# Two pairs of loads of a down projection are asked for before the last store of the up projection

## Chip, cores and metric

The kernel runs on one core of a Trainium2 chip. The metric is the device time of one execution in microseconds (us), as the median of several runs.

## The reference, cut to what matters

The function is one layer of a decoder trunk on 1024 positions of width 1024, in float32. A mixer with three branches comes first and is not touched here. The second half of the layer is a gated feed-forward block with a causal convolution over three positions:

```python
def conv_gated_ffn(h, w_up, conv_w, w_down):
    up = causal_depthwise_conv(h @ w_up, conv_w)
    gate, val = jnp.split(up, 2, axis=-1)
    return (jax.nn.silu(gate) * val) @ w_down
```

`w_up` is 1024 x 5632 and `w_down` is 2816 x 1024. The result is added to x.

## The kernel before, in words

The engines run their own programs and wait on each other by semaphores. TensorE (PE) multiplies. ScalarE (ACT) and VectorE (DVE) copy, scale and split. SyncE (SP) issues the transfers of this stage, in the order of its program, so a wait in SP's program holds every transfer behind it. Each float32 operand is split into a high part (ACT, a copy to the matmul's type) and a low part (DVE, the value less its high part), and each product is made of three matmuls: high by high, high by low, low by high.

**Up projection** (`UpProjection`). 2816 features are 22 tiles of 128, numbered 0 to 21 (`LAST` is 21). For each tile PE makes the products, ACT and DVE put the sums together, scale and convolve them (`convolve`, L1560 and L1563), ACT applies silu (`gate_silu`, L1509), DVE multiplies gate and value (`gate`, L1571), and SP stores the gated tile of 128 x 1024 in DRAM (`store`, L1444, to `scr_act`, 512 KB). The tail of a tile's work lies beside the products of the next tile.

**Down projection** (`DownProjection`). It has 44 steps: steps 0 to 21 make the left half of the output columns, steps 22 to 43 the right half. A step s takes one gated tile f = s mod 22 and 128 rows of half of `w_down`. `load` (L1614 to L1621) brings both from DRAM with two transfers of 512 KB and 256 KB, into the raw buffers `a_raw[s % 2]` and `w_raw[s % 2]`, so that there are two pairs of buffers. ACT and DVE split them: `split_a_hi` (L1637), `split_w_hi` (L1644), `split_a_lo` (L1648), `split_w_lo` (L1652), in two pairs of split buffers as well. PE then makes 24 matmuls (L1675 to L1677), three for each of eight banks of PSUM. The waits of a step are:

- `load(s)`, from step 2 on, waits until both low parts of step s-2 are made (the raw buffers are then free) and until the store of tile f has landed.
- `split_a_hi(s)` waits for the load, and from step 2 on until step s-2 has been multiplied.
- `step(s)` waits for the two low parts of step s.

After step 21 and step 43 DVE adds x, eight tiles of 256 KB that `load_x` (L1626) brings to `down_x`, and `write_out` (L1630) stores the result.

SP's program at the seam is, in order: the loads of steps 0 and 1, the store of tile 20, the store of tile 21, a wait for the last product of one kind of the up projection, eight transfers of x, and then the loads of steps 2, 3, 4 and so on. On ACT and DVE the splits of step 2 stand directly behind the convolution, silu and gate of tile 21.

Of the kernel before, what the change touches and what calls it, by code (L numbers as in the profile page):

```python
# [1371 lines left out]
def after(eng, sem, value):  # L1372

    if isinstance(value, int) and value <= 0:
        return
    eng.wait_ge(sem, value)


def looped(eng, first, last, body):

    body(0)
    with eng.Fori(first, last) as i:
        body(i)
# [296 lines left out]
def stage_combine_out_ffn(m):  # L1680
# [32 lines left out]
    down = DownProjection(m, up)  # L1713
# [13 lines left out]
    def tile_of(it, u):  # L1727
        return it * 2 + u // NB, u % NB

    with nc.Block() as block:  # L1730
        @block.sync
        def _(sp):
            def body(it):
                for u in range(UNITS):
                    d, n = tile_of(it, u)
                    after(sp, mul_done, it * UNITS + u - (UNITS - 1))
                    sp.dma_start(gate[u], gate_src[n][:, bass.ds(d, 1), :].rearrange("p a t -> p (a t)")).then_inc(gate_in[u], 16)
                    after(sp, lo_done, it * UNITS + u - 1)
                    sp.dma_start(raw[u % 2], branch_src[n][:, :, bass.ds(d * P, P)]).then_inc(w_in[u % 2], 16)
                    if isinstance(it, int) and u == 1:  # L1740
                        for k in range(2):
                            sp.dma_start(wo_raw[slot[k]], m.ins["w_out"][0, k * P:(k + 1) * P, :]).then_inc(wo_in[k], 16)
            looped(sp, 1, ITERS, body)
            sp.wait_ge(mul_done, ALL)
            sp.dma_start(rows, m.ins["x"][0].rearrange("(i p) d -> p i d", p=P)).then_inc(x_in, 16)
            for k in range(2, KD):
                if freed_by[k]:
                    sp.wait_ge(wo_lo_done, freed_by[k])
                if k == 4:
                    sp.wait_ge(sum_done, KD)  # L1750
                sp.dma_start(wo_raw[slot[k]], m.ins["w_out"][0, k * P:(k + 1) * P, :]).then_inc(wo_in[k], 16)
            sp.wait_ge(wo_lo_done, 4)
            up.load(sp, 0)
            for t in range(TT):
                sp.wait_ge(x_add, 2 * t + 2)
                sp.dma_start(m.scr_x[t * P:(t + 1) * P, :], rows[:, t, :]).then_inc(x_saved[t], 16)
            sp.wait_ge(out_mm, 2 * TT)
            up.load(sp, 1)
            for j in (1, 2, 3, 4):
                sp.wait_ge(t_lo[j], HK)  # L1760
            up.load(sp, 2)
            for i in range(1, LAST + 1):
                if i + 2 <= LAST:
                    sp.wait_ge(up.lo[4], i + 1)
                    up.load(sp, i + 2)
                if i == LAST:
                    for s in range(2):
                        down.load(sp, s)
                up.store(sp, i - 1)
            up.store(sp, LAST)  # L1770
            sp.wait_ge(up.mm[6], LAST + 1)
            for t in range(TT):
                down.load_x(sp, 0, t)
            for s in range(2, down.STEPS):
                down.load(sp, s)
                if s == down.FT + 1:
                    for t in range(TT):
                        down.write_out(sp, 0, t)
                if s == down.FT + 4:
                    for t in range(TT):  # L1780
                        down.load_x(sp, 1, t)
            for t in range(TT):
                down.write_out(sp, 1, t)
            sp.wait_ge(down.saved, 2 * TT * 16)
# [440 lines left out]
```

## Time and profile before

| what | value |
|---|---|
| median of 3 runs | 1687.22 us (1685.41 to 1688.19) |
| the profiled execution's own time | 1687.36 us |
| its span, from first to last instruction | 1685.6 us |
| mean granted TensorE clock over the span | 0.972 |
| PE matmuls | 7326, busy 1552.4 us (92% of the span) |
| DVE, ACT, GpSimd (POOL) busy | 870.1, 609.9, 123.0 us |
| transfers | 153.65 MB, mean 91 GB/s |

The times of instructions in the rows below are in microseconds from the start of the span. The clock is given as a share of the full 2.4 GHz. The share of DMA is the mean busy share of the core's 16 DMA engines.

### The profile page before, as it was taken

Reading aid. Unit: us, or ns where it says so; the run is one execution under the profiler, and the core shown is the slowest. Engines: PE = TensorE matmul, PEld = TensorE weight load, DVE = VectorE, ACT = ScalarE, POOL = GpSimd, SP = SyncE. Lnnn points to the kernel's source line nnn. Section 1 sums busy time; section 2 is a strip of 40 time slices with the busy share of each in tenths; the row PEclk is TensorE's granted clock in tenths of the full one; section 3 lists DMA queues with packets and bytes.
Section 4 is the critical chain, followed back from the end, with each engine's and each line's share of the span. In section 5 each row is a group of like instructions: output and inputs, shape, how many; then the busy total and the mean of one; then the engine's idle time right before and its main releaser. Section 6 shows DMA issues by size and latency. Waiting matters only on the chain. (4 is left out here: it accounts for less than half of the span.)

```text
span 1685.6 us, 19061 instructions
## 1 busy us (share of the span) xinstructions
PE 1552.4 (92%) x7326; PEld 1256.9 (75%) x7326; DVE 870.1 (52%) x1147; ACT 609.9 (36%) x997; POOL 123.0 (7%) x104
## 2 busy tenths in 40 slices
PE   5999999996989999885898978999999999799999
PEld 4899876665576676674677767888888888688887
DVE  4310343336275333873582547888778877333433
ACT  4310234441213453222451324555555555233222
POOL 1000230002041001200220000000000000000000
PEclk9999999998999999997899988999999999899999
DMA  5220230004122011210754112222223221544743
GB/s 189 72 90 1 65 91 26 25 26 134 34 63 69 26 32 37 92 36 10 252 187 159 75 50 63 89 87 88 76 76 99 76 88 63 178 147 150 244 139 141
DMA packets 126500, 153.65 MB, mean 91 GB/s; under 512 B 11530, under 2 KB 94397, under 8 KB 126141
## 3 DMA queue, kind: packets, MB, share of 16 engines
q1 hardware_dynamic: 126224, 152.40, 27.6%
q8 instruction: 57, 0.93, 0.2%
q14 instruction: 30, 0.25, 0.1%
q10 hardware_dynamic: 189, 0.08, 0.0%
HBM read 115.55 MB, written 36.31 MB: 90 GB/s over the span
## 5 line engine op out<-in xcount | busy, mean ns | idle before, releaser
L1586 PE MATMUL ps<-split_arena 128*128 128x512 f32 x1320 | 309.4, 391 | 3.3 <-DVE split_arena L2029 2.4
L489 PE MATMUL ps<-split_arena 128*128 128x512 f32 x1152 | 285.8, 400 | 27.9 <-ACT plain_arena L524 15.1
L1586 PEld LDWEIGHTS ps<-split_arena 128*128 128x128 f32 x1320 | 248.7, 189 | 56.1 <-DVE split_arena L2029 3.1
L489 PEld LDWEIGHTS ps<-split_arena 128*128 128x128 f32 x1152 | 213.5, 191 | 74.1 <-issue 26.1
L1675 PE MATMUL ps<-down_w,down_a 128*128 128x512 f32 x352 | 137.7, 391 | 10.6 <-DVE down_w L1652 10.6
L1676 PE MATMUL ps<-down_w,down_a 128*128 128x512 f32 x352 | 137.4, 390 | 0.0
L1677 PE MATMUL ps<-down_w,down_a 128*128 128x512 f32 x352 | 137.4, 390 | 0.0
L1586 PE MATMUL ps<-up_b,split_arena 128*128 128x512 f32 x528 | 130.0, 397 | 4.9 <-DVE split_arena L1514 4.9
L1648 DVE TENSOR_TENSOR down_a<-plain_arena,down_a 128x1024 fp32r<-128x1024 f32 x44 | 53.9, 1224 | 155.4 <-ACT down_a L1637 155.3
L1586 PEld LDWEIGHTS ps<-up_b,split_arena 128*128 128x128 f32 x528 | 101.5, 193 | 26.7 <-DVE split_arena L1514 5.2
L1637 ACT ACTIVATE down_a<-plain_arena 128x1024 fp32r<-128x1024 f32 x44 | 46.7, 1061 | 171.9 <-PE ps L1677 144.9
L690 DVE TENSOR_REDUCE stat<-ps 128x1 f32<-128x128 f32 (+3 forms) x64 | 48.4, 756 | 103.4 <-PE ps L617 103.3
L315 PE MATMUL ps<-split_arena 128*128 128x426 f32 (+1 forms) x256 | 94.0, 367 | 6.2 <-issue 2.6
L531 POOL TENSOR_TENSOR split_arena<-plain_arena,split_arena 128x1024 fp32r<-128x1024 f32 x24 | 59.4, 2474 | 498.1 <-ACT split_arena L513 498.1
L659 ACT ACTIVATE plain_arena<-ps,stat 128x128 f32<-128x128 f32 (+3 forms) x64 | 47.5, 743 | 131.0 <-DVE stat L690 131.0
L316 PE MATMUL ps<-split_arena 128*128 128x426 f32 (+1 forms) x256 | 92.4, 361 | 0.0
L317 PE MATMUL ps<-split_arena 128*128 128x426 f32 (+1 forms) x256 | 92.2, 360 | 0.0
L1675 PEld LDWEIGHTS ps<-down_w,down_a 128*128 128x128 f32 x352 | 66.4, 189 | 24.8 <-DVE down_a L1648 11.0
L2113 PE MATMUL ps<-split_arena 128*128 128x512 f32 x288 | 69.1, 399 | 16.9 <-POOL split_arena L2084 16.4
L614 PE MATMUL ps<-plain_arena 66*128 66x512 f32 (+5 forms) x192 | 78.1, 515 | 1.4 <-ACT plain_arena L670 1.4
L2113 PEld LDWEIGHTS ps<-split_arena 128*128 128x128 f32 x288 | 54.5, 192 | 31.9 <-POOL split_arena L2084 20.7
L636 PEld LDWEIGHTS ps<-plain_arena 128*64 128x64 f32 x576 | 61.2, 136 | 22.0 <-issue 22.0
(318 smaller groups left out, 2367.4 us busy)
## 6 DMA issues: line engine op xcount, KB each, us to landing
plain_arena<-scr_act SPq DMA_DIRECT2D x44, 512.0 KB, 3.6
plain_arena<-in_w_in SPq DMA_DIRECT2D x24, 512.0 KB, 4.0
scr_gate<-plain_arena SPq DMA_DIRECT2D x48, 256.0 KB, 2.0
plain_arena<-scr_gate SPq DMA_DIRECT2D x24, 512.0 KB, 4.3
plain_arena<-in_w_up SPq DMA_DIRECT2D x22, 512.0 KB, 5.2
up_raw<-in_w_up SPq DMA_DIRECT2D x22, 512.0 KB, 5.0
scr_act<-plain_arena SPq DMA_DIRECT2D x22, 512.0 KB, 2.6
plain_arena<-in_w_down SPq DMA_DIRECT2D x44, 256.0 KB, 3.9
```

Of the source, the lines that this page charges most:

```text
L315: nc.tensor.matmul(o, hi, wh, start=(k == 0), stop=False)
L316: nc.tensor.matmul(o, hi, wl, start=False, stop=False)
L317: mm = nc.tensor.matmul(o, lo, wh, start=False, stop=(k == KD - 1))
L489: mm = nc.tensor.matmul(m.ps[:, self.banks[half], :], w[:, k, :], src[:, k, h * BANK:(h + 1) * BANK], start=(j == 0), stop=(j == self.PER_ ...
L531: self.m.nc.gpsimd.tensor_tensor(self.w_lo[u % 2], self.raw, f32(self.w_hi[u % 2]), ALU.subtract).then_inc(self.lo, 1)
L614: mm = nc.tensor.matmul(S[n % 2][:, a:b], q_t[h % nb][0:kd, i * P:(i + 1) * P], k_t[h % nb][0:kd, a:b], start=True, stop=not diag)
L636: mm = nc.tensor.matmul(ps[rows, 6, (i % 4) * P:(i % 4 + 1) * P], v_of(h, j), pt_buf[n % 2][:, j * P:(j + 1) * P], start=(j == 0), stop=(j ...
L1586: mm = nc.tensor.matmul(o, self.w[j][w][:, k, :], self.h[j][k][h], start=(j in self.OPENS and k == 0 and n == 0), stop=(k == self.HK - 1 a ...
L1675: nc.tensor.matmul(o, a_hi[:, cut], w_hi, start=(f == 0), stop=False)
L1676: nc.tensor.matmul(o, a_hi[:, cut], w_lo, start=False, stop=False)
L1677: nc.tensor.matmul(o, a_lo[:, cut], w_hi, start=False, stop=(f == self.FT - 1)).then_inc(self.mm, 1)
L2113: mm = nc.tensor.matmul(proj_ps[u % 2][:, cut], w[:, k, :], src[:, 2 * n + k, cut], start=(k == 0 and w is hi and src is m.br_hi), stop=(k ...
```

## The change

SP's program asks for the loads of steps 2 and 3 directly behind the store of tile 20, ahead of the store of tile 21. The loop that held them before begins with step 4 for its loads. Nothing else is changed: each transfer has the same waits, buffers and bytes as before, and the programs of the other engines are the same.

```diff
                 up.store(sp, i - 1)
+            down.load(sp, 2)
+            down.load(sp, 3)
             up.store(sp, LAST)
             sp.wait_ge(up.mm[6], LAST + 1)
             for t in range(TT):
                 down.load_x(sp, 0, t)
             for s in range(2, down.STEPS):
-                down.load(sp, s)
+                if s >= 4:
+                    down.load(sp, s)
                 if s == down.FT + 1:
                     for t in range(TT):
                         down.write_out(sp, 0, t)
```

## Rows read from the trace of the kernel before

**Rows 1.** The page's first line, and the waits between 1441 and 1453 us: total, times, longest.

```profile
span 1685.6 us, 19061 instructions
...
ACT down_a L1637 <- DMA plain_arena<-scr_act: 13.1, 2, 12.8
```

**Rows 2.** Busy time by stretch: length, PE, PEld, DVE, ACT, POOL, clock, DMA share, GB/s.

```profile
1425.00:1434.00 9.00, 9.00 (x41) 7.47 (x40) 7.66 (x8) 4.02 (x5) 0.00 (x0) 1.00 0.14 58
...
1441.50:1452.20 10.70, 0.22 (x1) 0.00 (x0) 1.83 (x2) 2.60 (x4) 0.00 (x0) 0.66 0.86 317
1560.00:1575.00 15.00, 15.00 (x67) 12.41 (x67) 8.65 (x13) 4.15 (x6) 0.00 (x0) 1.00 0.77 262
```

**Rows 3.** Timeline of PE: start, duration, line, count, idle time before and its releaser.

```profile
1430.67 0.39 PE L1675 MATMUL ps<-down_w,down_a 128*128 128x512 f32 x1
...
1435.89 0.39 PE L1677 MATMUL ps<-down_w,down_a 128*128 128x512 f32 x1
...
1441.33 0.39 PE L1677 MATMUL ps<-down_w,down_a 128*128 128x512 f32 x1
1452.29 0.76 PE L1675 MATMUL ps<-down_w,down_a 128*128 128x512 f32 x1 [10.57 <-DVE down_w L1652]
...
1455.56 0.39 PE L1677 MATMUL ps<-down_w,down_a 128*128 128x512 f32 x1
```

**Rows 4.** The chain that ended last, at the seam: start, duration, what.

```profile
1436.49 1.24 DVE plain_arena L1571
1437.74 0.32 SPq L1444
1438.10 0.43 SPq L1626
...
1442.72 6.47 DMA plain_arena<-scr_act
1449.22 1.06 ACT down_a L1637
1450.31 1.23 DVE down_a L1648
1451.54 0.61 DVE down_w L1652
```

**Rows 5.** Timeline of all engines and of SP's queue, 1406 to 1453 us.

```profile
1406.17 0.43 SPq L1620 DMA_DIRECT2D plain_arena<-scr_act  x1
...
1411.24 1.06 ACT L1637 ACTIVATE down_a<-plain_arena 128x1024 fp32r<-128x1024 f32 x1 [1.54 <-DMA plain_arena<-scr_act]
...
1424.08 0.68 DVE L1652 TENSOR_TENSOR down_w<-plain_arena,down_w 128x512 fp32r<-128x512 f32 x1
...
1425.93 12.13 SPq L1444 DMA_DIRECT2D scr_act<-plain_arena  x2
1426.95 0.68 DVE L1652 TENSOR_TENSOR down_w<-plain_arena,down_w 128x512 fp32r<-128x512 f32 x1
...
1435.39 1.06 ACT L1509 ACTIVATE plain_arena<-plain_arena 128x1024 f32<-128x1024 f32 x1 [2.67 <-DVE plain_arena L1563]
...
1452.25 0.29 PEld L1675 LDWEIGHTS ps<-down_w,down_a 128*128 128x128 f32 x1 [10.96 <-DVE down_a L1648]
```

**Rows 6.** Timeline of ACT in the steady steps: step 4's split of the gated tile.

```profile
1459.47 1.06 ACT L1637 ACTIVATE down_a<-plain_arena 128x1024 fp32r<-128x1024 f32 x1 [6.72 <-PE ps L1677]
```

**Rows 7.** The loads of gated tiles (L1620), all 44, from issue to landing.

```profile
DMA to landing us min/median/max: 3.2/3.6/7.4
```

**Rows 8.** Timeline of ACT, DVE and PE at the start of step 24.

```profile
1570.12 1.06 ACT L1637 ACTIVATE down_a<-plain_arena 128x1024 fp32r<-128x1024 f32 x1 [5.71 <-DMA plain_arena<-scr_act]
...
1572.36 0.68 DVE L1652 TENSOR_TENSOR down_w<-plain_arena,down_w 128x512 fp32r<-128x512 f32 x1
...
1573.43 0.39 PE L1675 MATMUL ps<-down_w,down_a 128*128 128x512 f32 x1
```

## The prediction

> **What bounds the kernel now.** I read the span first, then the busy time by stretch, the waits and the chain of work that ended last around the seam, and the timeline last, for the order. PE is the engine at the end of the chain: in the stretches beside the seam it is busy all the time, 9.00 of 9.00 us and 15.00 of 15.00 us at clock 1.00, and from 1441.50 to 1452.20 us it is busy 0.22 of 10.70 us [rows 2]. So each us of PE's time there is a us of the kernel, and the question is only what ends this hole and what comes next. The waits show that ACT sat 12.8 us until a gated tile landed [rows 1], and the chain says why that tile was late: the gate of tile 21 ends at 1437.73, SP stores it, SP issues eight transfers of x from 1438.10 on, and only at 1442.72 is the tile of step 2 asked for; it lands 6.47 us later [rows 4]. Behind it come its splits, and PE restarts at 1452.29 [rows 3]. The reader is to see that nothing in step 2's load needs the gate of tile 21. It is late by its place in SP's program.
>
> **When the moved loads are issued and land.** The load of step 2 waits for the low parts of step 0; the last ends at 1424.08 + 0.68 = 1424.76. The load of step 3 waits for those of step 1, ready at 1426.95 + 0.68 = 1427.63. SP is free after the store of tile 20, which it issues at 1425.93 [rows 5]; this row holds two stores, and the second is that of tile 21 at 1437.74 [rows 4]. So the two transfers of step 2 go out near 1426.3, and those of step 3 near 1427.7, 10.0 us before SP has the next store to issue. Four issues of some 0.4 us each fit there, and the store of tile 21 and the x transfers keep their times. No wait is added for them. The landing is bounded by the fastest and the slowest of the 44 loads, 3.2 and 7.4 us [rows 7]; the nearest case is step 0's load, which also stood right behind a store of 512 KB, and was read by ACT 1411.24 - 1406.17 = 5.07 us after its issue [rows 5]. I take 5.1 us: step 2's tile is there at 1431.4 and step 3's at 1432.8, at the slowest at 1433.7 and 1435.1. The DMA engines have a share of 0.14 in that stretch, and that is the store [rows 2], so the 1.5 MB meet nothing else.
>
> **When the splits are made.** Both loads are now early, so other waits set them. ACT is in the silu of tile 21 until 1436.45 [rows 5], and step 0, whose last matmul starts at 1435.89 and runs 0.39 [rows 3], is then done. ACT splits step 2 at about 1436.5 (1.06 us for the tile, and some 0.6 for the weights). DVE comes free of the gate at 1437.73 and takes 1.23 + 0.61 us by its starts [rows 4], to 1439.6 at the latest. PE could start step 2 at 1439.7 and needs it at 1441.56, so 1.9 us are spare. If an early load cost DVE or ACT something in the convolution of tile 21, this is the cover. The splits of step 3 wait for the last matmul of step 1. In the steady steps ACT starts 0.5 us after the start of such a matmul: that of step 2 starts at 1455.56 + 15 x 0.227 = 1458.97, ACT at 1459.47 [rows 3, 6]. Here that gives 1441.8, with the low parts by 1441.8 + 3.1 = 1444.9, against PE's need at 1447.0. Spare 2.1 us, as in all steady steps.
>
> **What is removed.** 47 spacings from 1430.67 to 1441.33 give 0.2268 us for a matmul and 24 x 0.2268 = 5.44 us for a step [rows 3]. Without the hole step 2 starts at 1441.33 + 0.23 = 1441.56 instead of 1452.29: 10.73 us. The hole has a second price. The clock over it is 0.66, the mean of two levels, 2.4 GHz and 1.2 GHz [rows 2], and the first matmuls behind it are slow: the ninth of step 2 starts at 1455.56, 3.27 us after the first, where 8 x 0.2268 = 1.81 us are due [rows 3]. That is 1.46 us more. PE doesn't stop in the new order, so there is no reason for the fall; it ran at 1.00 through all the fully busy stretches [rows 2]. Together 12.19 us.
>
> The Trainium skill, page "TensorE: Matmul & The Clock Gate", Part 1 (the heading on 56 ns), puts back-to-back matmuls of 512 columns at 426.7 ns cold and 215.7 ns warm. By that, eight cold ones would cost 8 x 0.211 = 1.69 us in place of 1.46, and the gain would be 12.4 us; the trace has 226.8 ns warm, and 3.27 / 8 = 409 ns over those eight, so the rows' 1.46 stands.
>
> **What is late next: step 4.** This is the disputed point. The load of step 4 now stands where that of step 2 stood, behind the eight transfers of x. Its own waits (low parts of step 2, 1439.6) are over before SP comes to it at 1442.72, and the transfers ahead of it in the queue are the same ones at the same times. I take the same landing, 1449.22. The DMA engines are busy at a share of 0.86 until 1452.2 [rows 2], so this is the bandwidth, not the issue. Then ACT and DVE do what they did for step 2, and the weights of the first matmul can be loaded at 1452.25 [rows 5]. PE needs them at: step 4 due at 1441.56 + 2 x 5.44 = 1452.44, its weight load about 0.22 before that, 1452.22. The hole at step 4 is thus 0.03 us. Two steps of PE work (10.88 us) fit the lateness (10.73 us) almost exactly. Below, this can't go under zero, since PE is full; above, each us of later landing is a us of hole. If the landing took 7.4 us, the slowest in the trace, in place of 6.5 [rows 4, 7], it would be 0.9 us. The next load, step 5, is asked for when step 3's low parts are there, 1444.9, some 1.1 us later than the corresponding one of before; it may land as late as 1444.9 + 7.4 = 1452.3, and its split waits for step 3 anyway, until 1452.7. Nothing is late there. From step 6 on all loads hang on PE's own progress, as before.
>
> **Later places.** The same pattern stands at the half, where writes and x go ahead of step 24's load. There DVE is ready at 1573.04 for a matmul at 1573.43, 0.4 us spare [rows 8]. All of it is timed by PE, so it moves as a whole and costs nothing more. PE was also busy all through 1560 to 1575 with the DMA share at 0.77 [rows 2]: full queues beside PE don't slow it.
>
> **The sum.** 10.73 + 1.46 - 0.03 = 12.16 us. The profiled execution took 1687.36 us (span 1685.6), 0.14 over the median shown. 1687.36 - 12.16 = 1675.2, and against the median of 1687.22 it is 1675.1 us, 0.72% less.
>
> **Rivals.** (a) *A part of the wait comes back at step 4.* The x transfers and step 4's pair are on the edge: beyond a landing at 1449.4, 3.07 us of splits before 1452.44, every us counts fully, and a hole long enough brings the low clock and its 1.46 us too. Two us later would give 1677.1, with the clock 1678.5. For: no slack. Against: the same transfers in the same order, and the follower is later, not earlier. 10% for a loss of 1.5 us or more with a rest that is still faster.
> (b) *The wait is only moved.* If the load of step 4 is late by nearly the whole hole, the time stays near 1687. That needs a landing 9 us later, 15 us or more from issue where 7.4 is the longest seen [rows 7]. 4%.
> (c) *Slower.* One mechanism: x and the pair of step 4 are drawn out, with PE now reading and the queue deep, until step 4 lands past 1460.1; there hole and clock (10.7 + 1.46) eat the 12.19 us. At 1463.5, 20.8 us from issue, it is slower by 0.2%, 1690.6. Against it: rows 2 show no such effect with PE at work and queues at 0.77. 2%.
> (d) *The hole goes, the clock's refund doesn't*, if the clock falls for some other reason: 1675.1 + 1.46 = 1676.6. 2%.
> That the change doesn't do what it says would need SP to be held at step 3's wait; its condition is met at 1427.63, 10 us early.
>
> **From this to the numbers.** The forecast has 82%, (a) 10, (b) 4, (c) 2, (d) 2. A change within 0.2%, 3.4 us, can't be told from none. Faster: forecast, (a) and (d), 94%; same 4%; slower 2%. The runs of before reach from 1.8 us under to 1.0 us over their median. The low end is 1675.1 - 1.8 = 1673.3, as no term can give more; the high end 1678.5 takes in (a) with two us and the clock, and (d).
>
> **What would show it.** Right: the transfers of steps 2 and 3 issued near 1426.3 and 1427.7; the matmuls from L1675 on without a break at 1441.6, with the clock at 1.00; the store of tile 21 still at 1437.7 and step 4's load at 1442.7; a hole of at most 0.1 us near 1452.4; PE ending 12.2 us earlier. Wrong: a wait of ACT on a gated tile beyond 1449.4 with PE idle behind it, a hole at the half near 1561, or a gate of tile 21 later than 1437.7.

## The result and the profile after

The changed kernel takes 1673.82 us, the median of 6 runs (1669.62 to 1678.92), beside 1687.24 us for the kernel before (6 runs, 1684.93 to 1688.88). The ratio is 0.9918 with a 95% interval of 0.9904 to 0.9933, which is 11.3 to 16.2 us. The forecast was 1675.1 us in a range of 1673.3 to 1678.5.

The profiled execution has a span of 1667.9 us. Its down projection begins at 1423.13 where that of before began at 1430.67 [rows 3], in code that nothing was changed in, so times after and before are compared by their distance from there. SyncE's queue at the seam:

```profile
1418.05 0.32 SPq L1444 DMA_DIRECT2D scr_act<-plain_arena  x1
1418.49 0.35 SPq L1620 DMA_DIRECT2D plain_arena<-scr_act  x1
...
1419.83 0.34 SPq L1620 DMA_DIRECT2D plain_arena<-scr_act  x1
...
1430.19 0.32 SPq L1444 DMA_DIRECT2D scr_act<-plain_arena  x1
1430.56 4.67 SPq L1626 DMA_DIRECT2D down_x<-scr_x  x8
1435.36 0.36 SPq L1620 DMA_DIRECT2D plain_arena<-scr_act  x1
```

The two tiles are asked for behind the store of tile 20, the store of tile 21 keeps its place directly behind the gate, and step 4's tile stands where step 2's stood [rows 4]. ACT's timeline, the lines of the gated tiles of steps 2, 3 and 4:

```profile
1428.85 1.06 ACT L1637 ACTIVATE down_a<-plain_arena 128x1024 fp32r<-128x1024 f32 x1
...
1434.29 1.06 ACT L1637 ACTIVATE down_a<-plain_arena 128x1024 fp32r<-128x1024 f32 x1 [3.85 <-PE ps L1677]
...
1443.60 1.06 ACT L1637 ACTIVATE down_a<-plain_arena 128x1024 fp32r<-128x1024 f32 x1 [7.73 <-DMA plain_arena<-scr_act]
```

Step 2's split waits for nothing but ACT itself, step 3's for PE, as in every steady step, and step 4's for its transfer. PE's timeline:

```profile
1423.13 0.39 PE L1675 MATMUL ps<-down_w,down_a 128*128 128x512 f32 x1
...
1434.01 0.39 PE L1675 MATMUL ps<-down_w,down_a 128*128 128x512 f32 x1
...
1444.67 0.39 PE L1677 MATMUL ps<-down_w,down_a 128*128 128x512 f32 x1
1446.67 0.47 PE L1675 MATMUL ps<-down_w,down_a 128*128 128x512 f32 x1 [1.62 <-DVE down_w L1652]
```

Step 2 begins at 1434.01 without a break. Step 4 was due at 1444.67 + 0.23 = 1444.90 and begins at 1446.67, a hole of 1.77 us. The busy time by stretch shows the same, and that the clock stays up over so short a hole:

```profile
1434.00:1444.70 10.70, 10.70 (x49) 8.82 (x47) 1.83 (x3) 2.68 (x4) 0.00 (x0) 1.00 0.88 316
1444.70:1446.70 2.00, 0.38 (x3) 0.06 (x1) 1.94 (x3) 1.69 (x3) 0.00 (x0) 1.00 0.03 12
```

Against [rows 2], 10.70 us with 0.22 us of PE's work have become 10.70 us of 10.70. From the chain that ended last, the wait for step 4's tile, where [rows 4] have 6.47:

```profile
1435.36 8.22 DMA plain_arena<-scr_act
...
1443.60 1.07 ACT down_a L1637
```

**A yardstick.** From the start of the down projection's first matmul to the start of its last it is 251.33 us before (1430.67 to 1682.00) and 241.08 us after (1423.13 to 1664.21): 10.25 us less at the seam. The spans differ by 17.7 us; the other 7.5 us lie ahead of the seam. In the profiles of kernels that have no edit ahead of the seam that start lies between 1423.1 and 1431.3 us. Counted by matmuls, 7.1 of the 7.5 us arise between 730 and 1070 us. There the granted clock is 0.91 and 0.92 in the two profiles of the kernel before, and 0.93 or 0.94 in the seven profiles of kernels that have their edit at the seam. Why it is so isn't shown.

### The profile page after: what moved, and what is told of

Read it like the earlier page. It is cut to its first block and busy times, and to the rows that moved or that the text cites. A ratio compares the mean times of both kernels' runs of the same rounds, so it can differ in the third digit from the quotient of the medians.

```text
span 1667.9 us, 19061 instructions
## 1 busy us (share of the span) xinstructions
PE 1545.7 (93%) x7326; PEld 1251.3 (75%) x7326; DVE 870.1 (52%) x1147; ACT 609.9 (37%) x997; POOL 123.1 (7%) x104
## 5 line engine op out<-in xcount | busy, mean ns | idle before, releaser
L524 ACT ACTIVATE plain_arena<-ps 128x512 f32<-128x512 f32 x48 | 28.6, 597 | 134.7 <-DMA scr_gate<-plain_arena 87.2
```

## The experiments

All numbers of a profile are of one execution of that kernel. "Length" is the yardstick above, "landing" the time from the issue of the gated tile that stands behind the eight transfers of x to the start of ACT's split, and "packet" is explained with the fifth experiment.

**1. The changed kernel again.** No edit.

> The changed kernel once more. Theory (the hole before step 2 goes, what stays of it is set by the landing of step 4's gated tile behind the eight transfers of x): PE runs without a break from step 0 to step 3, and the hole at step 4 is between 0 and 2 us, by the landing alone: its size is the landing of step 4's tile (start of ACT's split) plus 3.07 us less the time at which step 4 is due. Rival (the 1.8 us of later landing in the first profile was chance): the landing is back near 6.5 us after the issue and the hole at most 0.2 us. Time 10 to 14 us under the kernel before in both.

1674.03 us against 1688.11, ratio 0.9927 (0.9910 to 0.9943). Length 240.56 us, landing 1447.46 - 1439.51 = 7.95 us, hole 1.25 us. So the late landing was not chance, and it sets the hole: landing + 3.07 us of splits, less the time at which step 4 is due.

**2. One pair only.**

```diff
+            down.load(sp, 2)
             up.store(sp, LAST)
...
-            for s in range(2, down.STEPS):
+            for s in range(3, down.STEPS):
```

> Only step 2's pair is moved ahead of the last store; step 3's pair stays behind the transfers of x. Theory (each pair moved covers one step of PE's work, 5.44 us, of the lateness): step 2 starts without a break, and a hole of about 5.3 us stands before step 3, with or without a fall of the clock (1.5 us): 5.3 to 7 us faster than before. Rival (one early pair is enough, since the queue then has less to do): the hole is under 2 us and the gain near 10 us or more.

1684.45 us, ratio 0.9979 (0.9966 to 0.9991), a gain of 1.5 to 5.7 us. Length 248.17 us, 3.16 us less than before. The start of step 3:

```profile
1451.69 0.76 PE L1675 MATMUL ps<-down_w,down_a 128*128 128x512 f32 x1 [6.08 <-DVE down_w L1652]
```

The hole has moved by one step and shrunk by less than one: 6.24 us where some 5.3 was expected, since the landing took 7.46 us. And the clock behind it cost 2.80 us (fourteen slow spacings) where 1.46 was the model: it was still at 0.50 from 1451.6 to 1457.4 us, 5.7 us beyond PE's restart, where in the kernel before it rose some 2.9 us beyond it, at 1455.2. The rival (one pair is enough) is out; the size of the gain was missed.

**3. Only the transfers of x moved.**

```diff
-            for t in range(TT):
-                down.load_x(sp, 0, t)
             for s in range(2, down.STEPS):
                 down.load(sp, s)
+                if 5 <= s < 5 + TT:
+                    down.load_x(sp, 0, s - 5)
```

> The loads of steps 2 and 3 stay behind the last store, but the eight transfers of x are issued one by one behind the loads of steps 5 to 12. Theory (two things stand before step 2's pair, the wait for the gate of tile 21 and the transfers of x): step 2's pair goes out at the time of the last store plus 0.4 us and lands 4 to 5 us later, so of the hole of 10.7 us some 3.5 to 5 us are left, with the clock's price or without: 6 to 8.5 us faster. Rival (the hole is the gate's alone): no more than 2 us faster.

1681.79 us, ratio 0.9967 (0.9955 to 0.9979), a gain of 3.5 to 7.6 us. Step 2's tile goes out 0.15 us after the end of the last store's issue and lands 4.72 us later:

```profile
1437.70 0.32 SPq L1620 DMA_DIRECT2D plain_arena<-scr_act  x1
...
1442.42 1.06 ACT L1637 ACTIVATE down_a<-plain_arena 128x1024 fp32r<-128x1024 f32 x1 [6.48 <-DMA plain_arena<-scr_act]
...
1445.48 0.76 PE L1675 MATMUL ps<-down_w,down_a 128*128 128x512 f32 x1 [4.28 <-DVE down_w L1652]
```

A hole of 4.44 us is left, as expected, and 2.88 us of slow clock (at 0.50 until 6.0 us beyond the restart). Length 246.45 us, 4.88 less than before, where 6 to 8.5 were expected: the clock was taken too cheap (the time's 6.3 us at the median is within it, by what lies ahead of the seam). Both things that stood ahead of step 2's pair are real: without x in front some 6.3 us of hole go, and the rest needs the pair ahead of the gate.

**4. The change with the transfers of x spread.** The changed kernel with the edit of the third experiment.

> The change, with the eight transfers of x issued one by one behind the loads of steps 5 to 12. Theory (the transfers of x ahead of step 4's pair are all that makes step 4 late): no hole at all from step 0 to step 21, step 4's tile landed 4 us or more before it is needed, 12.2 us faster at the seam and 0 to 2 us faster than the changed kernel. Rival (with PE at work the loads themselves land later, whatever stands ahead): loads of 7 us or more from issue remain and step 4 still waits.

1674.39 us, ratio 0.9926 (0.9910 to 0.9942). Length 239.13 us, 12.20 us less than before, with no hole in it. In the waits of the stretch from 1430 to 1460 us nothing waits for a transfer any more, and PE waits for nothing:

```profile
ACT down_a L1637 <- PE ps L1677: 15.4, 4, 3.9
DVE down_a L1648 <- ACT down_a L1637: 14.3, 4, 3.6
ACT plain_arena L1509 <- DVE plain_arena L1563: 2.7, 1, 2.7
DVE plain_arena L1571 <- ACT plain_arena L1509: 1.1, 1, 1.1
```

Step 4's tile lands 3.37 us after its issue, 4.3 us before ACT comes to it. What is ahead of step 4's pair is what made it late. The 1.4 to 2.0 us that this takes from the seam can't be seen in the time: 1674.39 and 1674.03 us, each with an interval of some 5 us. A second profile of the same kernel:

> The change with the transfers of x spread, once more. Theory: 239.1 to 239.3 us from the first to the last matmul of the down projection, no hole up to step 21, wherever the packet of instructions falls, since no queue is full beside step 4's pair. Rival: the first profile without a hole was chance, and a hole of 0.5 us or more is seen.

1673.91 us, one run. Length 239.35 us. There is no hole up to step 21, and 0.2 us were lost at the start of step 24, the thin place of [rows 8]. The words "wherever the packet falls" are not tested: in both profiles the packet came 0.3 us after step 4's tile had landed.

**5. The hole filled with matmuls.** The kernel before, with work put into PE's program (`again` issues the three matmuls of a bank once more).

```diff
             for s in range(down.STEPS):
+                if s == 1:
+                    pe.wait_ge(down.a_lo, s + 1)
+                    pe.wait_ge(down.w_lo, s + 1)
+                    for _ in range(2):
+                        for t in range(TT):
+                            down.again(pe, s, t)
                 down.step(pe, s)
```

> The kernel before, with PE repeating step 1's 24 matmuls twice ahead of step 1 itself, so that 48 matmuls more stand where the hole was; the output counts step 1's product three times. Theory (the clock's fall is a price of its own, 1.46 us, and comes from the hole): PE has no hole before step 2 beyond 0.2 us plus any later landing, clock 1.00 throughout, the ninth matmul of step 2 comes 1.8 us after the first instead of 3.3, and the time is 1.0 to 1.5 us under the kernel before although PE does 10.9 us more. Rival one (the clock would fall here anyway): same slow matmuls. Rival two (PE at work makes the transfers beside it later): step 2's tile lands 8 us after its issue in place of 6.5, as step 4's did in the first profile of the changed kernel, and PE waits 1.5 us or more for it.

1685.92 us, ratio 0.9989 (0.9977 to 1.0001), which can't be told from the kernel before, with 10.9 us more of PE's work. Length 251.56 us, where 251.33 was that of before. Step 2's tile lands 7.72 us after its issue, and PE waits:

```profile
1451.20 0.47 PE L1675 MATMUL ps<-down_w,down_a 128*128 128x512 f32 x1 [1.08 <-DVE down_w L1652]
...
1453.13 0.40 PE L1677 MATMUL ps<-down_w,down_a 128*128 128x512 f32 x1
```

The second row is the ninth matmul of step 2, 1.93 us behind the first, where [rows 3] have 3.27: with PE kept at work the clock doesn't fall. So its price belongs to the hole. What was to be gained by that, 1.46 us, went to the later landing: the second rival's number came out. Its reason had then to be tested, for between PE idle and PE at work one more thing differs. The queues between issue and landing, kernel before (1442.72 to 1449.22 us) first:

```profile
q1 hardware_dynamic: 1210, 2.59, 104.2%
```

and the changed kernel (1435.36 to 1443.60 us):

```profile
q1 hardware_dynamic: 1376, 3.01, 98.6%
q8 instruction: 1, 0.02, 0.8%
q14 instruction: 2, 0.02, 0.5%
```

The columns are packets, MB and their share of 16 engines' time. The one packet of q8 has 16384 bytes, and its 0.8% of 16 x 8.24 us is some 1.05 us on one of the 16 engines. In the kernel before the packet came at 1458.21 us, after the landing. Counted in PE's instructions it came at the same place in both kernels. The busy time from the start of the span to the packet, before first and the changed kernel below, has as many matmuls and weight loads in one as in the other, 12677 in all, some 40 beyond the end of step 1:

```profile
0.00:1458.21 1458.21, 1328.24 (x6338) 1071.63 (x6339) 786.88 (x1051) 546.63 (x917) 123.02 (x104) 0.97 0.25 80
0.00:1438.34 1438.34, 1321.06 (x6338) 1066.07 (x6339) 786.89 (x1051) 546.71 (x917) 123.10 (x104) 0.97 0.25 80
```

So these are PE's own instructions, asked for by their count: with the hole PE reaches that count after the landing, without it before. The Trainium skill, page "Runtime: NRT & Kernel Launch", Instruction fetch mechanics, says that a sequencer refills its instructions in blocks of 16 KiB (256 instructions) through a DMA queue of its own. The size of the packet agrees with it, and so does their number: the profile has 57 packets of q8 in the span, by the page 57 x 256 = 14592 instructions, near PE's own 14652 (7326 matmuls with as many weight loads).

The same can be read in the steady steps of the kernel before. Of the loads of gated tiles of steps 6 to 21 and 29 to 43, six have such a packet between issue and landing, and they took 4.08 to 5.58 us; the other 25 took 3.24 to 3.68 us. Step 9's tile and, with its packet, step 10's, each from a stretch of its own (the last number is us to landing):

```profile
plain_arena<-scr_act SPq DMA_DIRECT2D x1, 512.0 KB, 3.6
...
q8 instruction: 1, 0.02, 1.5%
...
plain_arena<-scr_act SPq DMA_DIRECT2D x1, 512.0 KB, 5.6
```

In all 13 profiles together, 74 of 78 such loads with a packet took more than 4 us, and 5 of 325 without one. A full queue is no condition for the delay.

**6. to 9. The packet moved by an edit elsewhere.** Small matmuls at the start of the output product, some 550 us ahead of the seam, shift the count of PE's instructions and nothing else at the seam. In the profile each call in the code is two matmuls with a weight load each, so PE has twice the instructions that the expectations count: 200 more for 50 calls, 48 for 12, 512 for 128 and 24 for 6.

```diff
             pe.wait_ge(mul_done, ALL)
+            for _ in range(50):        # also 12, 128 and 6
+                nc.tensor.matmul(ps[:, 7, 0:P], m.ident[:], m.ident[:], start=True, stop=True)
             for k in range(KD):
```

> The changed kernel with 50 small matmuls of PE more (100 instructions with their weight loads, on a bank that is written anew later) at the start of the output product, some 500 us ahead of the seam; nothing at the seam is edited. In the profiles in which step 4's pair landed late, one packet of 16384 bytes of the queue of instructions took 1.0 to 1.1 us on one DMA engine while the queue was full, and none did in the kernel before, where PE stood still. Theory (PE's own instructions are fetched over the same DMA engines, at fixed counts of them, and the engine that carries them finishes its share of step 4's tile last): 100 instructions more move that packet some 11 us earlier, ahead of the last store; step 4's tile lands about 6.5 us after its issue, the hole at step 4 is at most 0.3 us, and from the first to the last matmul of the down projection it is 239.1 to 239.4 us in place of 240.6 and 241.1. Rival (PE's reads at work slow the transfers): landing 7.5 us or more and a hole of 1 us or more, as before. The time as a whole is 0 to 6 us more than the changed kernel's, for the matmuls added.

1684.17 us, ratio 0.9974 (0.9960 to 0.9988), some 10 us over the changed kernel where 0 to 6 were expected. The padding was double, and PE was at it for 13.06 us:

```profile
883.42 13.06 PE L2157 MATMUL ps<-ident 128*128 128x128 f32 x100 [1.97 <-DVE plain_arena L1937]
```

The seam is as the theory has it. The packet comes at 1435.27 us, 11.8 us ahead of the last store; the tile is asked for at 1452.13 and read by ACT 6.38 us later; length 239.20 us. Timeline of ACT:

```profile
1458.51 1.06 ACT L1637 ACTIVATE down_a<-plain_arena 128x1024 fp32r<-128x1024 f32 x1 [5.79 <-PE ps L1677]
```

The row names PE, but the last matmul of step 2 starts at 1456.07 and runs 0.39 us, so it was over 2.0 us before. What ended the wait is the transfer, which landed 6.36 us after its issue. That was just in time for step 4. The busy time from the issue to ACT's start:

```profile
1452.13:1458.51 6.38, 6.38 (x30) 5.29 (x29) 1.83 (x2) 0.59 (x2) 0.00 (x0) 1.00 1.04 399
```

PE was busy in 6.38 of 6.38 us, so its work as such doesn't slow the transfers. The packet now stood beside the moved tile of step 2 instead, which landed after 6.42 us where eight other profiles have 4.3 to 5.0; that tile has time to spare.

> The same with 12 small matmuls (24 instructions). Theory (the fetch's place): the packet comes some 2.7 us earlier, still among the transfers of x, so that step 4's tile lands 7.4 to 8.3 us after its issue and PE waits 1 to 2 us for step 4. Rival (any such edit at the output product shifts the seam): the same landing as with 50 matmuls.

1677.80 us, one run. The packet moved by 8.7 to 9.0 us instead of 2.7, to 1438.99 us, 0.9 us ahead of the last store, so this was not the control it was meant to be. Twice the instructions make 5.4 us of it; the rest is that the count at which the packet comes isn't exact (12645 here, 12653 to 12677 in the nine profiles without padding). Landing 6.29 us, no hole at step 4, length 239.63 us with a hole of 0.38 us at step 24.

> The control that the run with 12 small matmuls was not: 128 small matmuls, 256 instructions of PE, which is the number that one packet of 16384 bytes holds at 64 bytes each, so that the packet is back at the same place of the seam as in the changed kernel. Theory (only the packet's place matters): it comes 2 to 4 us after the issue of step 4's pair, step 4's tile lands 7.4 us or more after its issue, PE waits 0.7 to 2 us, and the down projection's matmuls take 240 us or more. Rival (any padding of the output product cures it): landing under 6.6 us and 239.2 us.

1700.23 us, one run. The packet is back, 1.98 us after the issue; landing 7.31 us, hole 0.74 us, length 240.05 us. The expected 7.4 us was missed by 0.1, the rival's 6.6 by 0.7: padding alone cures nothing. That the packet came back although the padding was 512 instructions instead of 256 is luck: it is two packets' worth, and the profile has 59 packets of q8.

> 6 small matmuls, 12 instructions: the packet comes 1 to 5 us earlier than in the changed kernel, while the transfers of x fill the queue. Theory: late landing, 7.2 us or more, if the packet is at work after the transfers of x have begun to queue, some 3 us before the issue of step 4's pair or later; 6.6 us or less if it is ahead of them.

1677.85 us, one run. The packet comes 1.04 us after the issue; landing 8.15 us, hole 1.67 us, length 240.92 us. The waits between 1441 and 1456 us:

```profile
ACT down_a L1637 <- DMA plain_arena<-scr_act: 7.9, 2, 7.6
...
PE ps L1675 <- DVE down_w L1652: 1.5, 1, 1.5
```

**10. The kernel before again.**

> The kernel before once more, for its seam. Theory: no large packet of instructions between the last store and the landing of step 2's tile, landing 6.3 to 6.7 us after the issue, hole 10.4 to 10.8 us, and the slow clock behind it costs 1.5 to 2.9 us, by the time at which it rises. Rival (6.5 us was chance): landing 7.5 us or more with PE idle too.

1688.14 us, one run. Landing 6.46 us, no such packet, hole 10.78 us, length 251.53 us, of which 1.62 us are the slow clock.

All profiles in which eight transfers of x stand ahead of the tile, ordered by the packet's place (us from the tile's issue):

| kernel | packet | PE from issue to landing | landing | hole | length |
|---|---|---|---|---|---|
| 50 small matmuls | -16.9 | at work | 6.38 | none | 239.20 |
| 12 small matmuls | -6.0 | at work | 6.29 | none | 239.63 |
| before | +15.5 | idle | 6.50 | 10.73 | 251.33 |
| before, again | +14.9 | idle | 6.46 | 10.78 | 251.53 |
| 6 small matmuls | +1.0 | at work | 8.15 | 1.67 | 240.92 |
| 128 small matmuls | +2.0 | at work | 7.31 | 0.74 | 240.05 |
| one pair only | +2.2 | at work 4.4 us | 7.46 | 6.24 | 248.17 |
| hole filled | +2.5 | at work | 7.72 | 1.23 | 251.56 |
| changed, again | +2.7 | at work | 7.95 | 1.25 | 240.56 |
| changed | +3.0 | at work | 8.24 | 1.77 | 241.08 |

Six profiles with the packet among the tile's transfers have 7.31 to 8.24 us, four without 6.29 to 6.50 us. No profile has it between -6.0 and +1.0 or between +3.0 and +14.9 us, so where its effect begins and ends isn't shown. The two packets of q14 above are not the cause: the two padded kernels that landed in time have two as well, and the filled one, which landed late, has none.

## Why the prediction was right, and where it was off

**The bound and the cause.** Right. PE's hole was SP's order: with the two pairs ahead of the last store, steps 2 and 3 run without a break.

**Issue and landing of the moved loads.** Right. They go out 0.44 and 1.78 us behind the store of tile 20, against some 0.4 and 1.8 by the working, and land after 4.9 and 5.6 us, where 5.1 was taken. The store of tile 21 comes 12.14 us behind the store of tile 20, as it did before within 0.4 us (1437.74 - 1425.93 = 11.81 [rows 4, 5]), and no engine waits for the tiles. By the busy time of the stretch the DMA share rises from 0.14 [rows 2] to 0.70, and PE stays at 9.00 of 9.00 us:

```profile
1417.50:1426.50 9.00, 9.00 (x41) 7.48 (x40) 7.41 (x8) 4.02 (x5) 0.00 (x0) 1.00 0.70 233
```

**The splits.** Right. Step 2's low parts end at 1431.22 + 0.69 = 1431.91, 2.1 us ahead of the need at 1434.01, where 1.9 were worked out.

**The gain of 12.19 us.** Right, and measured without the other term by the spread version: 12.20 us less than before. Its two parts, the hole of 10.73 and the clock's 1.46, hold for the profile they were read from. The clock's part is no constant: behind holes of 10.78, 6.24 and 4.44 us it was 1.62, 2.80 and 2.88 us, by how long beyond PE's restart the clock stayed low.

**What is late next.** This is the term that was mis-sized. The place was right, and so was the rule (a landing beyond 1449.4 counts fully), but the step "I take the same landing" was off: 6.5 us was put in, 8.24 and 7.95 were measured, and the hole at step 4 is 1.77 and 1.25 us in place of 0.03. The argument given was that the same transfers stand ahead at the same times, and that full queues beside PE don't slow it. The second half looked at PE's side alone. The bound of 7.4 us for the loads was passed as well, by step 4's tile twice and by step 5's once (7.88 us; 7.37 in the second profile), which cost nothing behind the hole. The row for the landing came from a stretch in which PE was idle and asked for no instructions; the change makes PE work there, and its own packet of instructions then falls among the transfers. Moving that packet by an edit far off moves the landing between 6.3 and 8.2 us, which shows it as the cause. The trace of the kernel before could have told it: the longer ones among its steady loads are those with such a packet, and [rows 7] give only least, median and most. How it does so isn't shown. The rate of the 16 engines together doesn't explain it: between issue and landing they moved 370 GB/s against 399 before, but 402 with 128 calls, where the tile still landed 0.8 us later. So other transfers went past the tile while a part of it was late. That fits a single engine held up by the packet, but the rows don't name the engine of a packet, and that the delay (0.8 to 1.7 us over 6.5) reaches more than the 1.05 us of the packet is left open.

**The sum.** 12.16 us were worked out, the seam gave 10.25 and 10.77 us (lengths), and the time 13.4 us at the median, with an interval of 11.3 to 16.2 for the first measurement and 9.6 to 15.2 for the second. The second holds the seam's number; the first lies just above it. What is beyond the seam, some 3 us, is ahead of it, where nothing was changed. It need not be chance: in the four edited kernels of the experiments with nothing edited ahead of the seam the medians too gained more than the lengths, by 0.5 to 2.3 us, and all their profiles have the higher clock between 730 and 1070 us. No run here says why. So the forecast of the time, 1675.1 against 1673.82 and 1674.03, is nearer than its terms, and that is luck: 1.4 to 1.9 us too much at the seam and some 3 us ahead of it that the prediction didn't know.

**The rivals.** (a), a part of the wait back at step 4, is what happened, with a loss of 1.95 and 1.43 us against the 10% given to a loss of 1.5 or more (the second is just under it). Its hole didn't bring the low clock. (b), (c) and (d) did not come.

## What to carry to other kernels

When one queue issues in program order, look for loads whose own conditions are long met behind an item that waits for late work; moving them cost nothing here, where the issuer stood idle. Then put the next load in the order against its due time, and check what filled the queue in the row its landing is read from: a duration measured while the bounding engine stood still can be too short for the same transfer beside that engine at work, since packets of the engine's own instructions can then fall among the transfers. Look at the spread of like loads and at what the slow ones have in common before one of them is taken as the size. Bulk transfers that are needed much later (here x, needed 17 steps on) are better spread than placed ahead of loads with no slack: it took 1.4 and 1.95 us from the seam, which the time as a whole doesn't show. And count padding in the profile, not in the code.

## What the runs showed of the hardware

A single packet of 16384 bytes of instructions, about 1 us on one DMA engine, among some 4 MB of data that move in the same 13 us, makes a load behind the x transfers land after 7.3 to 8.2 us instead of 6.3 to 6.5 us; its place follows the count of PE's instructions, also of those executed 550 us earlier. A steady load of 512 KB, with nothing ahead of it, took 4.1 to 5.6 us instead of 3.2 to 3.7 in the kernel before when it met such a packet.

The clock's price behind a hole didn't grow with the hole: 1.46 and 1.62 us behind 10.7, 2.80 behind 6.24, 2.88 behind 4.44, and at most 0.2 us behind 1.2 to 1.8, where the granted clock stayed at 1.00. It follows when the clock rises: 2.9 and 3.2 us beyond PE's restart behind the holes of 10.7, 5.7 behind 6.24 and 6.0 behind 4.44.
